# Solve levels of a chunked linear attention: products of 64x64 quadrants in place of 128x128

## What is computed

```python
a = jnp.einsum('bhncd,bhnsd->bhncs', k_beta, k) * decay
a = jnp.where(strict, a, 0.0) + jnp.eye(CHUNK, dtype=f32)
rhs = jnp.concatenate([v_beta, k_beta * jnp.exp(g)[..., None]], axis=-1)
sol = lax.linalg.triangular_solve(a, rhs, left_side=True, lower=True, unit_diagonal=True)
```

## Time and profile before

| what | us |
|---|---|
| median of 3 runs (1582.12, 1582.59, 1586.21) | 1582.59 |
| the profiled execution | 1585.74 |
| its span, first to last instruction | 1583.9 |
| PE busy | 1547.6 |
| DVE busy | 1168.9 |
| ACT busy | 909.4 |
| L767 (y), 192 instructions | 22.4 |
| L777 (z), 192 instructions | 25.1 |

### The profile page before, as it was taken

How to read it: one execution, slowest core, us unless ns; L and a number is a source line. 1 busy time by engine, 2 the same in 40 slices (tenths; PEclk the granted TensorE clock), 3 DMA queues, 4 the chain that set the end, 5 groups by cost and what they waited for, 6 DMA issues and landing times.

```text
span 1583.9 us, 20558 instructions
## 1 busy us (share of the span) xinstructions
PE 1547.6 (98%) x8124; PEld 1299.0 (82%) x8124; DVE 1168.9 (74%) x1078; ACT 909.4 (57%) x841; POOL 70.6 (4%) x53
## 2 busy tenths in 40 slices
PE   7999998999999998999999999999999999999998
PEld 6899967999996566888888888888888888888886
DVE  4977444544453564988988988988988988988985
ACT  1353422433341353677677677677677677777763
POOL 1000010000001100000000000000000000000000
PEclk9999998999999997999999999999999999999999
DMA  5311276454545316999999999999999999999990
GB/s 202 117 55 54 83 261 257 177 196 175 197 173 200 110 51 234 377 379 359 390 382 361 392 382 356 394 378 358 395 381 354 396 383 355 393 383 359 392 384 28
DMA packets 186655, 445.60 MB, mean 281 GB/s; under 512 B 5485, under 2 KB 5637, under 8 KB 186592
## 3 DMA queue, kind: packets, MB, share of 16 engines
q1 hardware_dynamic: 182528, 430.52, 73.6%
q0 software_dynamic: 4064, 14.20, 3.1%
HBM read 437.86 MB, written 7.89 MB: 281 GB/s over the span
## 4 chain that ended last, share of the span: by engine, by line
PE 97%; ACT 1%; DVE 1%; DMA 0%; issue 0%; SPq 0%; POOL 0%; DVEq 0%; ACTq 0%; POOLq 0%
PE bank L1205 13%; PE bank L1207 13%; PE bank L1206 13%; PE bank L1192 6%; PE bank L1190 6%; PE bank L1191 6%; PE bank L605 4%; PE bank L667 4%; PE bank L913 3%; PE bank L915 3%; PE bank L914 3%; PE bank L1038 2%; PE bank L851 2%; PE bank L777 2%; PE bank L955 2%; PE bank L899 1%
## 5 line engine op out<-in xcount | busy, mean ns | idle before, releaser
L2058 DVE TENSOR_TENSOR ring_r<-ring,buf_r 128x2048 fp32r<-128x2048 f32 x336 | 751.5, 2286 | 32.0 <-ACT buf_r L1496 32.0
L1496 ACT ACTIVATE buf_r<-ring 128x2048 fp32r<-128x2048 f32 x336 | 629.3, 1915 | 52.3 <-PE bank L1192 43.4
L1205 PE MATMUL bank<-ring_r,buf_r 128*128 128x512 f32 x896 | 355.6, 397 | 0.5 <-DVE buf_r L2171 0.5
L1207 PE MATMUL bank<-buf_r,buf_r 128*128 128x512 f32 x896 | 350.3, 391 | 0.0
L1206 PE MATMUL bank<-buf_r,buf_r 128*128 128x512 f32 x896 | 349.7, 390 | 0.0
L1207 PEld LDWEIGHTS bank<-buf_r,buf_r 128*128 128x128 f32 x896 | 168.6, 188 | 36.3
L1205 PEld LDWEIGHTS bank<-ring_r,buf_r 128*128 128x128 f32 x896 | 168.8, 188 | 33.8 <-DVE buf_r L2171 0.6
L1206 PEld LDWEIGHTS bank<-buf_r,buf_r 128*128 128x128 f32 x896 | 168.8, 188 | 33.6
L1190 PE MATMUL bank<-ring_r,buf_r 128*128 128x512 f32 x448 | 175.9, 393 | 0.0
L1192 PE MATMUL bank<-buf_r,buf_r 128*128 128x512 f32 x448 | 174.6, 390 | 0.0
L1191 PE MATMUL bank<-buf_r,buf_r 128*128 128x512 f32 x448 | 174.3, 389 | 0.0
(11 more groups left out here) (300 smaller groups left out, 1738.6 us busy)
## 6 DMA issues: line engine op xcount, KB each, us to landing
ring<-in_moe_w_gate SPq DMA_DIRECT2D x56, 2048.0 KB, 8.5
ring<-in_moe_w_up SPq DMA_DIRECT2D x56, 2048.0 KB, 8.5
ring<-in_moe_w_down SPq DMA_DIRECT2D x56, 2048.0 KB, 8.8
ring<-in_a_w_in SPq DMA_DIRECT2D x8, 2048.0 KB, 9.1
ring<-in_dense_w_gate SPq DMA_DIRECT2D x7, 2048.0 KB, 9.2
ring<-in_dense_w_up SPq DMA_DIRECT2D x7, 2048.0 KB, 9.1
ring<-in_dense_w_down SPq DMA_DIRECT2D x7, 2048.0 KB, 7.9
ring<-in_a_w_out SPq DMA_DIRECT2D x2, 2048.0 KB, 8.8
```

The costliest lines, as they stand in the source:

```text
L1205: pe.matmul(o, xh, low[:, c], start=k == 0, stop=False)
L1207: ins = pe.matmul(o, xh, high[:, c], start=False, stop=k == KT - 1)
L1496: act.activation(HB[m % NHB], half_words(m, U_MOE), ACT.Copy).then_inc(m_wh, 1)
L2058: dve.tensor_tensor(half_low(m, U_MOE), half_words(m, U_MOE), HB[m % NHB], ALU.subtract).then_inc(m_wl, 1)
```

## The change

Each product of y and z in levels 1 to 5 is made as two products of 64x64x64, of the lower and the upper diagonal quadrant (rows, weight columns and moving columns 0 to 63, then 64 to 127). Both write the same bank, each its own 64 partitions. In level 6, y is one product (rows 0 to 63, weight columns 64 to 127, moving columns 0 to 63) and z another (rows 64 to 127, weight columns 0 to 63, moving columns 64 to 127). The subtraction on DVE is done on the quadrants alone, as two instructions of 64 partitions x 4 x 64 elements, and as one in level 6. The copies of y, the transposes and the mask products stay as they are.

```diff
             def turn(lv):
...
-                        m = pe.matmul(quad(g, i), X[0][:, u, :], R[4][:, u, :], start=True, stop=True)
+                        for z in (low, top) if lv < NLEV - 1 else (low,):
+                            c = z if lv < NLEV - 1 else top
+                            m = pe.matmul(quad(g, i)[c, z], X[0][z, u, c], R[4][z, u, z], start=True, stop=True)
                     m.then_inc(y_mm, 1)
...
-                        m = pe.matmul(quad(4 + g % 2, i), X[3][:, u, :], R[3][:, u, :], start=True, stop=True)
+                        for z in (low, top) if lv < NLEV - 1 else (top,):
+                            c = z if lv < NLEV - 1 else low
+                            m = pe.matmul(quad(4 + g % 2, i)[c, z], X[3][z, u, c], R[3][z, u, z], start=True, stop=True)
                     m.then_inc(z_mm, 1)
...
             def level(lv):
                 for g in range(4):
                     dve.wait_ge(z_mm, 4 * (lv - 1) + g + 1)
-                    dve.tensor_tensor(R[3][:, quads(g), :], R[3][:, quads(g), :], as_quad(4 + g % 2), ALU.subtract
-                                      ).then_inc(u_ready, 1)
+                    half = [slice(0, P // 2), slice(P // 2, P)]
+                    for z, c in zip(half, half) if lv < NLEV - 1 else [(half[0], half[1])]:
+                        r = R[3][z, quads(g), c]
+                        last = dve.tensor_tensor(r, r, as_quad(4 + g % 2)[z, :, c], ALU.subtract)
+                    last.then_inc(u_ready, 1)
```

More of the change, by code:

```diff
@@ L743, in _ @@
             project(6)
+            HP = P // 2
+            low, top = slice(0, HP), slice(HP, P)
             def turn(lv):
```

## The result

The changed kernel took 1590.84 us (median of nine runs, 1588.33 to 1594.01) beside 1584.32 us of the kernel before (nine runs, 1582.12 to 1587.91). The ratio is 1.0039, with a 95% interval of 1.0028 to 1.0050: slower by 6.2 us, 4.4 to 7.9. The forecast was a gain of 4.4 us.

What follows compares the result with a forecast made beforehand. PE bounds the kernel, with 97% of the chain that ended last. Gains of 0.2 (levels 1 and 2), 2.6 (levels 3 to 5) and 1.6 us (level 6) sum to 4.4, so 1582.6 becomes 1578.2 us; range 1575.5 to 1588.5.

Steps and rivals of the forecast that it cites:

- The size of a quadrant pair: y and z on PE, levels 1 to 5: two quadrant products side by side take 60 ns; a full instruction, 112.
- the first rival: Halves writing one PSUM bank don't overlap on PE, a pair costs 112 ns: 1582.5 us; chance 20%.
- the third: Each handover between halves drains PE's array, 0.16 us each, about 50 us in all: 1630 us; chance 4%.
- y and ACT's copy: Levels 3 to 5: y shrinks from 3.57 to 2.0 us, but z awaits ACT's copy, so 0.29 of 1.55 count.
- The other engine: DVE's subtraction in two halves, levels 1 to 5: 0.67 us per group instead of 0.60, 1.3 us more in all.
- Clock 1.00 throughout: Sign that the forecast is right: PE's granted clock stays at 1.00 throughout.
- rival 2: TensorE's clock falls as PE idles around z; slower from two falls on; chance 16%, two thirds of it slower than before.
- at three it is 1588.5: Three clock falls of 6.9 us, each costing about 3.4, take the time from 1578.2 to 1588.5 us.
- one counter-example: Evidence against clock falls: 16 matmuls of 8 moving columns (L1048), for 1.7 us from 588.16, ran at 1.00.
- Levels 1 and 2: y of level 1 gains nothing, waiting for ACT; DVE is busy up to level 2's subtractions; together 0.2 us gained.
- Level 6: z falls from 3.79 to 2.45 us, a gain of 1.34; y gains 0.29.
- the 1.6: Gain of y and z together in level 6: 1.6 us.

Runs made afterwards that it cites:

- the filled kernel: The changed kernel with unread products of 512, 256 and 384 columns in PE's idle gaps of levels 1 to 5: 1584.45 us, 0.9993 of the kernel before.
- the run with the same half twice: Kernel before, subtraction of levels 2 and 3 in four 64-partition instructions (lower twice, upper twice), levels 4 and 5 in two; 2.27 us from group to group.

## Why the prediction was wrong, point by point

**The size of a quadrant pair: right.** 64 products of y in 2.08 us are 32 pairs; single starts give 58 ns from pair to pair against the 60 taken. The fear of the first rival, that halves writing one bank run one after the other, fell with it, and so did the third, 0.16 us at each handover. Here the rows of after disagree with the rule of the Trainium skill (TensorEngine Tiling (Array Packing), Restrictions and Gotchas, Gotcha 1), at least for halves that write different partitions of the bank: the two starts of a pair stand 7 ns apart, and a pair takes no longer than the single quadrant product of level 6, 58 ns.

**y and ACT's copy: right.** 3.16 for y and its wait, forecast 3.28; the idle PE behind y was 1.08, forecast about 1.3.

**The other engine: the step that failed first.** The prediction took a half at 0.33 from a trace in which a tensor-tensor of 128x512 starts every 0.60, and got 1.27 for a group. Two instructions over 128 partitions do give 1.27. The halves over different partitions gave 1.61, with steps of 0.43 and 0.46 and 0.72 for the mask product. Its sum had 1.3 us more on DVE over the five levels; it was 0.41 x 20 = 8.2, of which 3.8 reached the time where only this was changed. In z of level 4, 0.34 of the 0.43 that was missing is this term; the rest is the last half's own 0.10. The rule quoted above was not weighed: the prediction asked in which bank the halves land, for PE, and not in which partition they start, for DVE.

**"Clock 1.00 throughout": the step that failed second, and the larger.** The sum put the clock at nothing; it cost about 7 us. This is rival 2, which had 16%. Its price per instruction was right: 16 instructions ran in 3.35 us instead of 1.79. Its "at three it is 1588.5" lies near the measured time by luck. It counts three falls of 6.9 us more than before, and the profile of after has 20.4 us at half clock where before has 6.8, so two more; the mean clocks of the executions speak for somewhat more than two. The 3.8 us of DVE's halves, which rival 2 doesn't have, fill the place of the rest. What was wrong was to weigh it at 16% on one counter-example, matmuls of 8 columns over 1.7 us, which stood between dense work. The idle time itself, 1.08, 0.63 and 0.93 us per level, was in the prediction as 1.3 and twice 0.7. The first failed step feeds this one: the last gap grew from 0.52 to 0.93 by DVE's longer steps, and with whole subtractions the levels had no fall.

**Levels 1 and 2: the kind right, the size not.** They hang on DVE, as said. From y of level 1 to the next work took 8.37 us (8.27 before), level 2 7.49 (7.76), but what was saved there was lost again in DVE's queue and in a fall. From the start of level 1 to that of level 3 it is 33.92 us, 32.28 in before, and 33.56 in the filled kernel, which has no fall there: 1.3 us lost at full clock, where the sum had 0.2 gained.

**Level 6: nearly right at full clock.** Forecast 2.45 for z, measured 2.32 where the clock held, 3.14 and 3.60 where a fall lay in it. So the 1.6 came as 1.1 (interval -0.6 to 2.7) when level 6 was changed alone.

**The sum, made again from runs.** Quadrants with whole subtractions -5.1 us (forecast for the whole change -4.4); DVE's halves +3.8, measured alone; the falls +7, the distance from after to the kernel with filled gaps. Together +5.7, where +6.2 was measured. The three come from different kernels and each has an interval of about 1.5 us, so the agreement is fair and not exact. Told the other way, the filled kernel (halves on DVE, one fall in the stretch like the kernel with whole subtractions) stands 4.0 us above the latter, where the halves alone cost 3.8; these are the same runs, and no second proof.

**What stays open.** Which gap brings a fall. In levels like 4, with 1.08, 0.47 and 0.52 us idle, there was none up to 163 us; with 1.08, 0.63 and 0.93 there were four falls in after and five in its sister with level 1 whole. But the length alone doesn't decide: with whole products, z's gaps of 0.68 and 1.01 us in level 3 had a fall behind them, and gaps of 0.81 and 1.15 us in two levels of the run with the same half twice had none. Each of these is one profiled execution. Also open is why the profiles of before and after show only 1.4 of 6.2 us in the stretch; after has 3.7 us there over the filled kernel, where the timed distance is 7. The execution of after that was profiled was one of the faster ones of nine. And what sets the fall at 178 us in before.

## What to carry to other kernels

When an instruction is split over partitions, look at where each part and its neighbours start: a part that starts at another partition than the last read of the same memory or the last write gives up the overlap, here at all three steps of a group, and a form that starts at partition 0 throughout had none of it. When work is taken off the bounding engine but its waits stay, ask what fills the gaps before counting the gain: here the gaps cost more in clock (about 7 us) than the shorter matmuls brought (5.1). Independent work moved into them, the projection, gained 9.2 us with the shorter matmuls and 5.7 without any.

## What the runs showed of the hardware

- Two 64x64x64 fp32 products in opposite quadrants, with their outputs in different partitions of one PSUM bank, start 7 ns apart, and the next pair starts 58 ns after; a single quadrant product with nothing beside it costs the same 58 ns.
- On DVE, consecutive fp32 tensor-tensors that start at the same partition overlap: steps of 0.60 us for a duration of 0.69 (512 elements), 0.33 for 0.41 (256). Where the start partition changes against the last read of the same memory or the last write, the next one starts only when the one ahead has ended: steps of 0.69 to 0.73 and 0.42 to 0.46.
- In the kernel whose TensorE stood idle for 1.9 us ahead of z in level 1 and for 1.08, 0.63 and 0.93 us in level 4, the granted clock fell to 1.2 GHz four times in 108 us, for 3.4 or 6.8 us at a time; with unread products in those gaps it stayed at 2.4 GHz for 84 us and the kernel was 7 us faster.
- A product of 512 fp32 columns is two instructions of 0.43 us each.
